# First block of a two-layer transformer step: convolution columns ahead of the projection, taps and modulation slabs spread over it, ring buffers by a table of releases, constants in two loads

## What is computed

```python
mod = jax.nn.silu(c) @ mod_w[i] + mod_b[i]          # i = 0, 1: 2 x 1024 x 6144
hx = _modulate(_rmsnorm(x, ln1_g[i]), sh1, sc1)     # the same for ctx with modc

def _mixer_ab(...):                                 # both token sets
    px = hx @ w_in                                  # 1024 x 1792: 512 q, 128 k, 128 v, 1024 for the convolution
    qx = _rope(_rmsnorm(_heads(px[..., :o_k], A_HEADS), q_g), cos, sin)
    kx = _rope(_rmsnorm(_heads(px[..., o_k:o_v], A_KV_HEADS), k_g), cos, sin)
    ox = _dense_attn_blocks(...)                    # 8 heads of 64, 2 kv heads
    bx = _conv_module(px[..., o_u:], ...)           # below
    yx = jnp.concatenate([_merge(ox), bx], axis=-1) @ w_out

def _conv_module(u, ...):
    a, gate = jnp.split(u, 2, axis=-1)
    glu = a * jax.nn.sigmoid(gate)
    y = depthwise_conv(glu, conv_w) + conv_b        # 31 taps, 512 channels
    return jax.nn.silu(layernorm(y))
```

## Time and profile before

| | us |
|---|---|
| median of 3 runs (lowest, highest) | 2475.91 (2474.61, 2482.41) |
| the profiled execution, its own time | 2481.54 |
| its span in the profile | 2479.8 |
| first matmul of the projection | 39.59 |
| first scores of the attention | 145.68 |
| mean of the convolution (behind the attention) | 267.82 |
| TensorE busy over the span | 2283.8 (92%) |
| VectorE busy over the span | 1113.8 (45%) |

### The profile page before, as it was taken

One profiled execution on the slowest core, in us unless ns is written; L12 is line 12 of the kernel. 1 busy time (PEld: TensorE's weight loads), 2 busy tenths in 40 slices (PEclk: granted clock), 3 DMA queues, 4 the chain that ended last, 5 costly groups with the idle time before them and its releaser, 6 DMA issues.

```text
span 2479.8 us, 30977 instructions
## 1 busy us (share of the span) xinstructions
PE 2283.8 (92%) x12196; PEld 1434.3 (58%) x12196; DVE 1113.8 (45%) x2040; ACT 547.9 (22%) x1054; POOL 13.4 (1%) x20
## 2 busy tenths in 40 slices
PE   6999968999999888878999999988999999899998
PEld 2544434444333347464444444378888988888997
DVE  2379442111111125632222222346688776568876
ACT  3223231111111113421111111122331002333101
POOL 0000000000000010000000000000000000000000
PEclk9999889999999999799999999979999999999999
DMA  9169116997999993125999999942244555224443
GB/s 384 68 274 427 73 41 261 373 376 312 420 386 421 428 392 155 68 102 220 411 424 421 426 417 427 395 162 83 100 157 166 181 186 206 100 92 163 163 177 119
DMA packets 48842, 629.86 MB, mean 254 GB/s; under 512 B 5616, under 2 KB 6512, under 8 KB 11248
## 3 DMA queue, kind: packets, MB, share of 16 engines
q1 hardware_dynamic: 43712, 611.28, 61.0%
q10 hardware_dynamic: 2880, 9.44, 0.9%
q0 software_dynamic: 2160, 7.87, 0.8%
HBM read 614.41 MB, written 14.16 MB: 253 GB/s over the span
## 4 chain that ended last, share of the span: by engine, by line
PE 78%; DVE 10%; DMA 6%; ACT 4%; issue 2%; SPq 0%; DVEq 0%; ACTq 0%
PE ps L1399 9%; PE ps L1451 9%; PE ps L1528 5%; DMA ring<-in_ex_up 5%; PE ps L1063 5%; PE ps L1529 5%; PE ps L1530 5%; PE ps L1430 5%; PE ps L1467 3%; PE ps L1355 3%; PE ps L1534 3%; PE ps L1535 3%; PE ps L1536 3%; PE ps L1293 3%; DVE cat L1932 2%
## 5 line engine op out<-in xcount | busy, mean ns | idle before, releaser
L1530 PE MATMUL ps<-hn_hi,w_lo 128*128 128x256 f32 x992 | 283.0, 285 | 0.0
L1451 PE MATMUL ps<-ring,E 128*64 128x512 f32 x1152 | 258.9, 607 | 17.5 <-DMA ring<-in_ex_up 16.0
L1399 PE MATMUL ps<-ring,E 128*64 128x512 f32 x1024 | 228.4, 599 | 3.1 <-SPq L576 3.1
L1451 PEld LDWEIGHTS ps<-ring,E 128*64 128x64 f32 x1152 | 87.6, 140 | 185.5 <-issue 184.0
L1530 PEld LDWEIGHTS ps<-hn_hi,w_lo 128*128 128x128 f32 x992 | 192.7, 194 | 0.0
L2170 DVE TENSOR_TENSOR E<-E,ps 128x512 f32<-128x512 f32 x18 | 12.4, 688 | 372.5 <-PE ps L1451 372.5
L1399 PEld LDWEIGHTS ps<-ring,E 128*64 128x64 f32 x1024 | 72.9, 138 | 141.5 <-issue 138.0
L1528 PE MATMUL ps<-hn_hi,w_hi 128*128 128x256 f32 x512 | 146.6, 286 | 2.4 <-DVE hn_lo L2291 2.4
L1529 PE MATMUL ps<-hn_lo,w_hi 128*128 128x256 f32 x512 | 146.1, 285 | 0.0
L1528 PE MATMUL ps<-hn_hi,w_lo 128*128 128x256 f32 x480 | 140.9, 294 | 5.4 <-DVE E L2368 3.7
L2259 DVE TENSOR_TENSOR w_lo<-ring,w_hi 128x4096 fp32r<-128x4096 f32 x32 | 141.6, 4425 | 1.1
(11 more groups left out here) (467 smaller groups left out, 3810.1 us busy)
## 6 DMA issues: line engine op xcount, KB each, us to landing
ring<-in_ex_gate SPq DMA_DIRECT2D x64, 2048.0 KB, 13.0
ring<-in_ex_up SPq DMA_DIRECT2D x64, 2048.0 KB, 14.4
ring<-in_ex_down SPq DMA_DIRECT2D x64, 2048.0 KB, 10.8
ring<-in_w_layer SPq DMA_DIRECT2D x56, 2048.0 KB, 8.0
ring<-in_w_static SPq DMA_DIRECT2D x33, 2048.0 KB, 11.0
y_rows<-E ACTq DMA_DIRECT2D x36, 256.0 KB, 8.6
E<-in_w_layer SPq DMA_DIRECT2D x2, 2048.0 KB, 12.5
cat<-in_w_layer SPq DMA_DIRECT2D x2, 2048.0 KB, 16.9
```

Source lines behind the costliest of these rows:

```text
L1399: ins = pe.matmul(ps[half(u), 2 + w, :], xg[:, k, half(u)], slab(2 * w + u, (KC, DE))[:, k, :], start=k == 0, stop=k == KC - 1)
L1451: ins = pe.matmul(ps[half(u), 2 + w, :], xg[:, k, half(u)], slab(2 * w + u, (KC, DE))[:, k, :], start=k == 0, stop=k == KC - 1)
L1530: return pe.matmul(out, lo, xhi, start=False, stop=last)
```

## The change

1. **Constants in two loads.** `CONSTS` is reordered so that `eps` and `fold` come first. The first loads are the first 128 columns of `par`, the first 33 of `con` and `xT` (`n_in = 3`). The other 2,237 columns of `con`, 816 of `par` and the positions (256 columns) follow behind the first slab of the projection and count on `cmp_in`. VectorE's casts, mask and angle tables (`tables`) move behind the first modulation; the sines move behind the first chunk.
2. **Order of the projection.** The columns of `w_in_ab` are permuted in the weight file (`AB_CHUNKS`): the eight convolution chunks first, then k, the four of q, and the values last.
3. **Modulation slabs.** Slabs 4 to 17 are summed one behind each of the 14 chunks, 18 to 23 in rounds 1 to 6 of the attention.
4. **Taps.** 46 behind the first two gated channels, 10 behind the other two, 4 beside each of the five norms of q and k, and 2 in each of 24 rounds.
5. **Norm and rotation** are split (`qk_scale`, `qk_rope`). The rotation of the last q chunk stands in round 3; the swap matmul behind the thirteenth chunk.
6. **Ring.** `AB_LOADS` gives the order of loads, `AB_FREED` the order in which buffers come free; a load takes the buffer of the slab freed six places earlier.

```diff
+AB_CHUNKS = (6, 7, 10, 11, 8, 9, 12, 13, 4, 0, 1, 2, 3, 5)
...
+        MOD_PLACE = ((5, 0, 8), (4, 0, 16), (7, 0, 24))
+        IN, OUT = 24, 28
...
+        AB_LOADS = [0, 1, 2, 3, IN, 4, 5, 6, IN + 1, 7, 8, 9, 10, IN + 2, 11, 12, 13, 14, IN + 3, 15, 16, 17, 18, 19, 20, 21, 22, 23, OUT, OUT + 1]
+        AB_FREED = [0, 1, 2, 3, 4, 5, 6, IN, 7, 8, 9, 10, IN + 1, 11, 12, 13, 14, IN + 2, 15, 16, IN + 3, 17, 18, 19, 20, 21, 22, 23, OUT, OUT + 1]
...
-            sp.dma_start(con[:, :], consts_in).then_inc(inputs_in, 16)
-            sp.dma_start(par[:, :], params_in).then_inc(inputs_in, 16)
+            sp.dma_start(par[:, 0:par_head], params_in[:, 0:par_head]).then_inc(inputs_in, 16)
+            sp.dma_start(con[:, 0:con_head], consts_in[:, 0:con_head]).then_inc(inputs_in, 16)
             sp.dma_start(xT[:, :, :, :], xT_in).then_inc(inputs_in, 16)
-            sp.dma_start(E[:, 0:NX].bitcast(I32), pos_in).then_inc(inputs_in, 16)
...
+                    if x == IN:
+                        sp.dma_start(con[:, con_head:n_con], consts_in[:, con_head:n_con]).then_inc(cmp_in, 16)
+                        sp.dma_start(par[:, par_head:n_par], params_in[:, par_head:n_par]).then_inc(cmp_in, 16)
+                        sp.dma_start(pos.bitcast(I32), pos_in).then_inc(cmp_in, 16)
...
+                    for n in range(14):
+                        if n % 4 == 0:
+                            w = take_ab(IN + n // 4)
+                        if n == 5:
+                            pe.wait_ge(cmp_in, 16 * late_in)
+                            pe.wait_ge(setup_done, 2)
+                        bank_free(n)
+                        if n == 13:
+                            values(w, P)
+                        else:
+                            mm_chunk(ps[:, n % 4, :], w, n % 4 * P, normed if n == 0 else lambda k: hsrc(True, k)).then_inc(proj_mm, 1)
+                        if n >= 10:
+                            qrot(n - 10, QK_ORDER[n - 10])
+                        if n >= 9:
+                            qss(n - 9, QK_ORDER[n - 9], 512)
+                        mod_sum(MOD0 + n)
+                        if n == 9:
+                            mod_columns(1)
+                        if n == 12:
+                            pe.wait_ge(rope_ready, 2)
+                            pe.matmul(ps[:, 4, :], cc("swap"), qk[:, QC, :], start=True, stop=True).then_inc(swap_mm, 1)
+                    pe.wait_ge(swap_ev, 1)
+                    pe.wait_ge(proj_ev, 14)
+                    pe.wait_ge(rope_ready, 4)
...
-                    if full and 1 <= s <= 24 - MOD0:
-                        if s == 9:
-                            mod_columns(1)
-                        mod_sum(1 if s < 9 else 2, MOD0 + s - 1)
-                    if full and s == 22:
+                    if full and 1 <= s <= 6:
+                        mod_sum(MOD0 + 13 + s)
+                    if full and s == 9:
                         mod_columns(2)
...
                 if full:
+                    gated(0)
+                    gated(1)
+                    tap(46)
+                    gated(2)
+                    gated(3)
+                    tap(10)
+                    for g, c in enumerate(QK_ORDER):
+                        qk_scale(g, c, 512, pc("qn_a" if c < QC else "kn_a"))
+                        if g == 1:
+                            modulation_second()
+                        tap(4)
+                        if g < 4:
+                            qk_rope(g, c)
...
-                    for _ in range(5):
-                        ins = next(taps, None)
-                        if ins is not None:
-                            step(ins, 1)
+                    if full:
+                        tap(2 if s < 24 else 0)
```

More of the change, by code:

```diff
@@ L542, in expert_stream, with static_loads @@
+            def static_loads(stream):
+                for r, (src, shape, _used) in enumerate(stream):
+                    sp.dma_start(slab(r, shape), src).then_inc(slab_in[r], 16)
+                sp.wait_ge(h_ready, 3 * KC)
+                sp.dma_start(invcnt, invcnt_in).then_inc(invcnt_ready, 16)
             def expert_stream(l, before):
                 sems = moe[l]
[L546 to L551, removed]
+                for r, (s, v) in before:
+                    w, u = r // 2, r % 2
+                    sp.wait_ge(s, v)
+                    src, shape = expert_loads(l, (0, NE - 1)[u])[w]
+                    sp.dma_start(slab(r, shape), src).then_inc(guess_in, 16)
@@ L1202, in block1 @@
                     bank_free(9)
[L1203 removed]
+                    values(w1, P)
                     qrot(g0 + 3, 3)
@@ L1220, in block1 @@
                 for s in range(len(units) + lag + 1):
+                    if full and s == 3:
+                        qrot(4, QK_ORDER[4])
+                    if full and s == 18:
+                        pe.wait_ge(rope_ready, 5)
                     if s < len(units):
@@ L1946, in block1 @@
                     modulation_first()
+                    tables()
                 else:
@@ L1957, in block1, with tap, gated @@
                     norm_group(3, 1)
[L1958 to L1966 removed]
+                taps = conv_taps() if full else iter(())
+                def tap(count):
+                    for _ in range(count):
+                        step(next(taps), 1)
+                def gated(c):
+                    dve.wait_ge(proj_ev, c // 2 * 4 + 3 + c % 2)
+                    g = gpad[:, c, :, HALO:HALO + NX]
+                    link(dve.tensor_tensor(g, g, g2(cat[:, 4 + c, :]), ALU.mult))
+                if full:
+                    gated(0)
[11 more added lines that the diff above has]
+                            qk_rope(g, c)
+                else:
+                    for c in range(QKC):
+                        qk_scale(g0 + c, c, 512 if c == QC else w, pc("qn_c" if c < QC else "kn_c"))
+                        qk_rope(g0 + c, c)
                 units = attention_units(layer)
                 for s in range(len(units) + 1):
+                    if full and s == 3:
+                        qk_rope(4, QK_ORDER[4])
                     if s < len(units):
@@ L2552, in static_slabs @@
 def static_slabs(a):
+    import numpy as np
     out = [rows_of(a["mod_w"][j // 12], j % 12 * 512, 512) for j in range(24)]
-    out += [rows_of(a["w_in_ab"][0], 512 * j, 512 if j < 3 else 256) for j in range(4)]
+    w = a["w_in_ab"][0]
+    w = np.concatenate([w[:, P * c:P * c + P] for c in AB_CHUNKS], axis=1)
+    out += [rows_of(w, 512 * j, 512 if j < 3 else 256) for j in range(4)]
     out += [rows_of(a["w_out_ab"][0], 512 * j, 512) for j in range(2)]
```

241 lines of the change are left out of this document (114 added, 127 removed).

## The result

The changed kernel takes 2535.24 us (median of 4 runs, 2530.0 to 2538.48) against 2478.51 us of the kernel before on the same chip (4 runs, 2474.61 to 2482.41): a ratio of 1.0227 with a 95% interval of 1.0201 to 1.0253, 56.7 us slower. The profiled execution took 2538.48 us of its own, its span is 2536.8 us, and the mean granted clock of TensorE fell from 0.957 to 0.938. The forecast was 2523 us, at most 2532: right in direction and in kind, too small by 12.

A forecast was written before the change was run, and what follows sets the result against it. TensorE bounds the projection; in slabless attention rounds TensorE and VectorE take turns and the clock falls. The mean of the convolution moves from 267.8 to 315.0, +47 on the median 2475.9, giving 2523 us, range 2498 to 2532.

The forecast's parts named there:

- The serial round: Attention rounds without a slab: TensorE's 2.65 us plus 1.76 between scores and transposes, 4.41 at full clock, 6.65 at 1.2 GHz.
- The clock is low in most rounds: Rounds 7 to 23: 10 to 16 steps at the 1.2 GHz level, 2516 to 2532 us; chance 0.65.
- Nor does this kind of work bring the clock back: Second block's attention in the earlier trace: clock stayed 0.50 through 13 us with TensorE busy 12.91.
- 13 of the 16 steps at that clock and 3 at full: Round 7 to round 23: 13 steps of 6.65 us and 3 at full clock, 86.5 + 13.2 = 99.7 us.
- The tail: From round 23's scores to the mean of the convolution: 10.3 us at low clock, 6.6 at full.
- Constants: Start: slab 3 lands 4.0 us earlier, sines and table load save 0.3; projection starts at 35.3, -4.3.
- Projection: 14 slabs of 1.9 us come in; projection takes 132.6 us instead of 106.1, first scores at 167.9, +22.2.
- Door: Entry to attention: last q norm delays first maximum to 173.4, first transposes to 177.0 (+24.9); TensorE idles over 5 us, clock falls.
- Behind the mean: After the mean of the convolution: only durations that stood before, so no further difference.

The follow-up runs named there:

- run 3: Changed kernel plus three unread matmuls between scores and transposes in attention rounds 7 to 12 only; 2520.74 us (one run).
- run 2: Changed kernel plus two unread matmuls over 384 columns between scores and transposes in rounds 7 to 23; 2497.72 us, ratio 1.0086 to the kernel before.
- run 4: Changed kernel plus two unread matmuls over 384 columns between scores and transposes from round 13 on; 2511.86 us, ratio 1.0124 to the kernel before.
- run 8: Changed kernel with transposes two units behind the scores instead of one, and a third PSUM bank; 2467.27 us, ratio 0.9958 to the kernel before.
- run 5: Changed kernel with modulation slabs 4 to 23 back in attention rounds 1 to 20; 2478.37 us, ratio 0.9981 to the kernel before.
- run 6: Changed kernel with 30 taps moved from the projection into the rounds, five each up to round 14; 2535.83 us, ratio 1.024 to the kernel before.
- run 10: Changed kernel with transposes two units behind scores, slabs 4 to 23 back in rounds, five taps in rounds 0 to 14; 2468.46 us, ratio 0.9954 to kernel before.
- run 1: Changed kernel plus three unread 512-column matmuls between scores and transposes in rounds 7 to 23; 2513.85 us, ratio 1.0135 to the kernel before.

## Why the forecast was right in kind and short in size

- **The serial round** was right. The open round is 4.38 and 4.49 us at full clock in run 3 (4.41 forecast) and 6.64 to 6.79 at 1.2 GHz (6.65); rounds 3 to 6 are 4.54 on average (4.55). From the end of the scores' step to the transposes it is 1.71 where I took 1.76, and 1.64 of it is idle.
- **"The clock is low in most rounds"** was right, and the runs show its cause. That the gap fells it, and not the smaller share of slabs or something in the program's place, is shown by runs 2, 3, 4 and 8: the clock falls when the gap opens and holds or returns when it is closed. The Trainium skill ("TensorE: Matmul & The Clock Gate", section "Why this matters for your kernels") asks only that TensorE not idle between bursts of matmuls for longer than any of these gaps. The traces do not agree that this is enough: the clock fell at gaps of 1.64 us, one in each round.
- **"Nor does this kind of work bring the clock back"** was a misreading. The stretch 1005 to 1018 us of the earlier trace rows ends too early; the kernel before goes on with

```profile
1019.48 1.97 PE L1263 MATMUL ps<-E 128*64 128x128 f32 x8
...
1024.40 1.12 PE L1233 MATMUL ps<-E 64*128 64x512 f32 x2
```

so the same kind of work is back at full clock by 1024, 6 us later (1.00 from 1025 to 1035). It is the gap that keeps the clock low in rounds 7 to 23, and not the kind of matmul. The page was also read too narrowly: the clock is lowest in slices 5 and 6 only within the first block; slices 17 and 27 have a 7.

- **The step that failed: "13 of the 16 steps at that clock and 3 at full".** The clock fell inside the first open round, at 209.9, and did not come back before 319: 15 steps were low and the first one half. From the scores of round 7 (206.65) to those of round 23 (312.39) it took 105.7 us, where the forecast had 99.7 + 1.0: 5 us short. Two more low steps are 4.5 of it, the first step 0.9 (5.29 instead of 4.41), the low steps 0.7 (6.70 on average instead of 6.65); `mod_columns` gave its 1.0 back, since it lay in the gap. The tail gave back 1.1, so the stretch missed by 4.0. No row stood behind the 3. The nearest one, 246.8 to 254.1 in the earlier trace rows, is a round and a half in which the clock stayed full, behind 85 us in which TensorE was busy 97%. In run 3, behind rounds in which it was busy 34.00 of 34.00, the clock holds into the third open round. In the changed kernel, which has the idle 5.47 us at the door 30 us earlier, it does not. That door is not the reason: in run 5 the idle 6.65 us lie 94 us back, TensorE was busy 79.72 of 80 us in between (160 to 240), and the clock falls in the first open round all the same:

```profile
246.70 0.66 PE L1335 MATMUL ps<-con,E 128*128 128x128 f32 x4 [1.76 <-DVE E L2048]
247.29 1.82 PE L1292 MATMUL ps<-E 128*64 128x128 f32 x8
```

Why it is the first open round in one kernel and the third in another stays open.

- **Constants**: 36.17, forecast 35.3. Slab 3 came 3.0 us earlier and not 4.0. The slabs' row starts 0.65 earlier (3.80 instead of 4.45, one load fewer to issue) and is 2.3 shorter (25.34 instead of 27.68), where the 1.69 MB taken out at 423 GB/s should have made it 4.0 shorter. So the first megabytes are not worth the rate of the full stretch; why not stays open. The start of the projection also depends on the clock: in the nine other runs with this split slab 3 lands between 29.11 and 29.52, and the first chunk starts between 34.62 and 37.28, as the sum of slab 3 takes 1.92 (run 2) to 3.64 us (run 6).
- **Projection**: 134.4 us, forecast 132.6. A chunk behind a slab takes 7.06 and not 6.87; 11 of them are 2.1 us, and the other terms came out 0.3 lower. I had priced the slab by its own rows and had counted nothing for what follows it. In the rounds of the earlier trace rows the same slab had cost 0.15, since it lay in the gap; so moving a slab out of a round into the projection costs 1.85 + 0.19 and saves little. That is the part of the loss that the clock does not explain: in run 2 the first transposes stand 27.2 us later than before (179.37), and from there to the mean it takes 104.9 us instead of 115.7, which gives back only 10.8.
- **Door**: first maximum 176.25 (forecast 173.4), first transposes 179.87 (177.0), round 7 at 206.65 (204.0). Nearly the whole error is the 2.7 us that it inherits; the idle time of over 5 us (5.47) and the fall of the clock came as said.
- **Behind the mean** I had nothing; the distance grew from 53.8 there to 57.0 at the end. In the pages the clock of the changed kernel is lower by one or two tenths in slices 7, 19 and 35 too. This is within the scatter of one execution to the next: the work behind the mean is the same in all runs, and it lasts from 2205.7 us (run 8) to 2215.2 (the changed kernel) in the profiled executions, 2212.0 before.

The errors together: 0.9 + 1.8 + 4.0 = 6.7 up to the mean, 3.1 behind it, and 2.6 because the median of the kernel before rose by that much with its fourth run: 12 of 12.

## What to carry to other kernels

Work that lies in a gap which two engines leave each other is free there and costs its full price elsewhere; before it is moved, compute the round without it, not only the rounds' sum of busy times. If that round has TensorE and another engine in turn, put one more unit of distance between producer and consumer first: here it took a third PSUM bank for the scores, turned +54 us at the mean of the convolution into -12, and decided whether moving taps was worth nothing or 8 us. And where the engine's clock can fall, a gap has a second price: here 37 us on top of 16.

## What was not expected of the hardware

- Short, repeated gaps were enough for the 1.2 GHz level: with 1.63 to 1.77 us of idle time in a round of 4.4 the granted clock fell within one to three rounds (the changed kernel, runs 3 and 5), and in the changed kernel it then stayed at 0.50 for 109.2 us with TensorE busy 84.10 of them.
- It came back when the gap was closed, with matmuls that nobody reads (0.50 in 240 to 250 us, 0.99 in 250 to 260, run 4) and with the attention's own transposes, values and scores (at 319 us in the changed kernel, at 185 in run 10).
- A full-array float32 matmul over 512 columns took 0.89 us (2.68 for three, run 1), a scores matmul with 64 rows over as many 1.05; a chunk costs 0.19 more when a slab with its 32 output rows stands ahead of it (7.06 against 6.87).
